# First memory piece split in the last layer's tail, next weights of block 2 shared out anew between engines; head and attention stages reordered

## What is computed

```python
for l in range(DEPTH):
    h = rms_norm(x, norm1_g[l]) * (1.0 + scale1) + shift1
    proj = h @ w_in[l]                    # latents c_q, c_kv, k_rope, and conv_u
    attn_out = mla_group(...)             # 4 heads, head norm, rope, softmax
    conv_out = conv_group(conv_u, ...)    # 31 taps by channel, layer norm, silu
    x = x + gate1 * (concat([attn_out, conv_out]) @ w_out[l])
    h2 = rms_norm(x, norm2_g[l]) * (1.0 + scale2) + shift2
    x = x + gate2 * expert_choice_ffn(h2, ...)   # 16 experts, 64 tokens each
```

## Time and profile before

| | us |
|---|---|
| median of 3 runs | 2667.12 |
| lowest and highest | 2662.14 and 2667.64 |
| the profiled execution | 2660.37 |
| its span | 2658.7 |

### The profile page before, as it was taken

The page is one execution under the profiler, slowest core; times in us unless marked ns, Lnnn a source line. Parts: engine busy times, 40 slices in busy tenths (PEclk is TensorE's granted clock), DMA queues, the critical chain, the costliest instruction groups (busy, mean ns, idle before and its releaser), DMA issues. The chain is left out here.

```text
span 2658.7 us, 31859 instructions
## 1 busy us (share of the span) xinstructions
PE 2481.6 (93%) x12913; PEld 1488.4 (56%) x12913; DVE 1124.8 (42%) x1732; ACT 851.1 (32%) x1161; POOL 298.8 (11%) x126
## 2 busy tenths in 40 slices
PE   6989799999997989799999998999999999989998
PEld 5734533333335735533333337887788777756665
DVE  4985312222223985312232225547521112356765
ACT  4245111111114245111111116556532234245553
POOL 0002000000000011000000005000244323300000
PEclk8999899999998989899999998999999999979999
DMA  9702579999999602499999995422223321149995
GB/s 339 273 1 83 203 303 409 410 409 410 409 408 329 225 1 95 191 353 409 410 410 410 410 402 148 149 89 80 80 74 97 131 80 48 48 176 371 358 353 207
DMA packets 276596, 650.48 MB, mean 245 GB/s; under 512 B 12144, under 2 KB 110718, under 8 KB 276222
## 3 DMA queue, kind: packets, MB, share of 16 engines
q1 hardware_dynamic: 273310, 638.87, 64.0%
q0 software_dynamic: 2592, 7.87, 0.8%
q10 hardware_dynamic: 576, 2.10, 0.2%
HBM read 641.99 MB, written 8.39 MB: 245 GB/s over the span
## 5 line engine op out<-in xcount | busy, mean ns | idle before, releaser
L790 PE MATMUL ps<-ring,scr 128*64 128x512 f32 x1952 | 426.9, 595 | 1.3 <-DMA ring<-in_w_up 1.3
L790 PEld LDWEIGHTS ps<-ring,scr 128*64 128x64 f32 x1952 | 138.9, 137 | 279.5 <-issue 274.6
L812 PE MATMUL ps<-ring,scr 128*64 128x512 f32 x1024 | 230.2, 603 | 1.4 <-ACT scr L1004 1.4
L1525 POOL TENSOR_TENSOR raw_r<-raw,w_high 128x2048 fp32r<-128x2048 f32 (+1 forms) x39 | 173.6, 4459 | 469.6 <-ACT w_high L1790 469.6
L1546 PE MATMUL ps<-x_high,w_high 128*128 128x512 f32 x464 | 187.5, 404 | 9.9 <-DVE y L2183 5.5
L1548 PE MATMUL ps<-x_high,raw_r 128*128 128x512 f32 x464 | 185.1, 399 | 0.0
L1547 PE MATMUL ps<-xT_r,w_high 128*128 128x512 f32 x464 | 184.5, 398 | 0.0
L1078 DVE SCALAR_TENSOR_TENSOR one_hot_T<-h_tok,convw,one_hot_T 128x512 f32<-128x512 f32 x240 | 170.5, 766 | 1.7
L490 POOL TENSOR_TENSOR one_hot_T_r<-hy,one_hot_T_r 128x1024 fp32r<-128x1024 f32 x16 | 38.5, 2404 | 1118.2 <-ACT one_hot_T_r L1016 1118.2
L1287 DVE TENSOR_TENSOR scr<-scr,ps 128x512 f32<-128x512 f32 x32 | 22.0, 688 | 314.6 <-PE ps L790 314.6
L2661 DVE TENSOR_TENSOR ring_r<-ring,ring_high 128x2048 fp32r<-128x2048 f32 x56 | 127.7, 2289 | 61.3 <-ACT ring_high L2539 61.2
(11 more groups left out here) (555 smaller groups left out, 4450.0 us busy)
## 6 DMA issues: line engine op xcount, KB each, us to landing
ring<-in_w_down SPq DMA_DIRECT2D x64, 2048.0 KB, 15.0
ring<-in_w_up SPq DMA_DIRECT2D x62, 2048.0 KB, 18.1
ring<-in_w_gate SPq DMA_DIRECT2D x60, 2048.0 KB, 14.7
ring<-in_w_up SPq DMA_DIRECT2D x56, 1024.0 KB, 7.7
ring<-in_w_ada SPq DMA_DIRECT2D x22, 2048.0 KB, 13.0
ring<-in_w_down SPq DMA_DIRECT2D x28, 1024.0 KB, 7.4
raw<-in_w_in SPq DMA_DIRECT2D x24, 1024.0 KB, 5.1
raw<-in_w_in SPq DMA_DIRECT2D x20, 512.0 KB, 4.7
```

Source lines behind the costliest of these rows:

```text
L790: mm = pe.matmul(ps[CAP * half:CAP * (half + 1), 1 + j // 2, :], x_e[:, at_x:at_x + CAP], weights[:, k, half * HALF:(half + 1) * HALF], st ...
L812: mm = pe.matmul(ps[CAP * half:CAP * (half + 1), 4, :], hidT[:, at_f:at_f + CAP], weights[:, k, half * HALF:(half + 1) * HALF], start=(j = ...
L1525: pool.tensor_tensor(dst, src, high.bitcast(F32), ALU.subtract).then_inc(w_ready, 1)
```

## The change

Seven things are done.

1. `TAPS_IN_TILE` has 1 and 5 taps where it had 4 and 2 (after input tiles 9 and 10). The 24 taps of the head stage become 16 before the ropes and 8 after them; `TAPS_IN_STEP` becomes 3, 3, 2, 4, 3, 4, 2.
2. Head stage on TensorE: the rotations move in between the last key tiles, into banks 4, 5, 0; the sums are taken in the order 0, 2, 3, 1, only the last waiting for all ten tiles; the value tiles are spread around the turning of the norms and the first key factor. ScalarE gets one dummy square root.
3. Attention: VectorE only inverts the row sum (new semaphore `inv_ready`); ScalarE scales the probabilities, after the exponential of the next step. The key factor and key norm come behind the inversion.
4. Nine matmuls of output tile 6 are done ahead, around the last transpose.
5. Tail of the last layer: the first four pieces are loaded in the order 0 to 3, ScalarE makes the high part of piece 0 there and GpSimd its low part, in place. VectorE no longer subtracts it in `second`.
6. Low parts in `second`: GpSimd 1 to 5, VectorE from 6 on. `w_ready` counts one less.
7. Piece 9's high part is made after the first of the four late key/value evictions instead of after all.

The core of the diff:

```diff
-TAPS_IN_TILE = (0, 5, 9, 9, 10, 10, 10, 10, 6, 4, 2, 4)
-TAPS_IN_HEADS = 24
-TAPS_IN_STEP = (4, 4, 4, 3, 3, 3)
+TAPS_IN_TILE = (0, 5, 9, 9, 10, 10, 10, 10, 6, 1, 5, 4)
+TAPS_IN_HEADS = (16, 8)
+TAPS_IN_STEP = (3, 3, 2, 4, 3, 4, 2)
+EARLY_OUT = 6
...
+def first_halves(M):
+    return M["ring2_r"][:, 3 * TT * D - 2 * SLOT:3 * TT * D - SLOT], M["h_tok_r"][:, 0:SLOT]
...
-    for i in (2, 3, 0, 1):
+    for i in range(SLOTS):
...
             with pool.If(l > DEPTH - 2):
+                pool.wait_ge(kv_split, 1)
+                pool.tensor_tensor(kv_low, h_tok[:, 0:SLOT], kv_high.bitcast(F32), ALU.subtract)
...
+                if i == 6:
+                    pe.wait_ge(qk_ev, 5)
+                    rotate(0, ROT_BANKS[0])
+                if i == 7:
+                    pe.wait_ge(qk_ev, 6)
+                    rotate(1, ROT_BANKS[1])
+            pe.wait_ge(qk_ev, 7)
+            rotate(2, ROT_BANKS[2])
...
-            for n in range(4):
+            for n in (0, 2, 3, 1):
+                if n == 1:
+                    pe.wait_ge(qk_ev, 10)
...
+            pe.wait_ge(roped, 3)
+            value_tile(0)
             pe.wait_ge(head_root, 1)
             for t in range(TT):
                 mm = pe.transpose(ps[:, 7, t * P:(t + 1) * P], head_rms[:, t * P:(t + 1) * P], ident)
             mm.then_inc(head_cols, 1)
+            value_tile(1)
+            value_tile(2)
...
             key_factor(0)
+            pe.wait_ge(qk_ev, 11)
+            value_tile(3)
...
                 j = i - 2
+                if j == 4 * HEADS - 1:
+                    early_output(0)
+                    early_output(1)
...
+                if j == 4 * HEADS - 1:
+                    early_output(2)
...
+                if 1 <= i <= 4 * HEADS:
+                    act.wait_ge(inv_ready, i)
+                    act.activation(prob[:, (i - 1) % 3, :], prob[:, (i - 1) % 3, :], ACT.Copy, scale=rrs[:, i - 1:i]).then_inc(prob_ready, 1)
...
             with act.If(l > DEPTH - 2):
+                act.wait_ge(ahead["slot_in"][0], 16)
+                act.activation(kv_high, h_tok[:, 0:SLOT], ACT.Copy).then_inc(kv_split, 1)
...
-                j = i - 1
-                if j >= 0:
-                    dve.wait_ge(exp_done, j + 1)
-                    step(dve.reciprocal(rrs[:, j:j + 1], rsum[:, j:j + 1]))
-                    step.settle()
-                    dve.tensor_scalar(prob[:, j % 3, :], prob[:, j % 3, :], rrs[:, j:j + 1], None, ALU.mult).then_inc(prob_ready, 1)
+                if i >= 1:
+                    dve.wait_ge(exp_done, i)
+                    dve.reciprocal(rrs[:, i - 1:i], rsum[:, i - 1:i]).then_inc(inv_ready, 1)
...
-            for i in range(1, KV_BEFORE + 1):
-                pool.wait_ge(w_ready, i)
+            for i in range(1, KV_BEFORE):
+                if i >= 2:
+                    pool.wait_ge(w_ready, i - 1)
...
-                    for i in range(2 * KV_BEFORE, 16):
+                    kv_kept(2 * KV_BEFORE)
+                    ahead(CH_H[1] - AHEAD)
+                    for i in range(2 * KV_BEFORE + 1, 16):
...
-            low_of(0)
...
-            next_low = [KV_BEFORE + 1]
+            next_low = [KV_BEFORE]
```

More of the change, by code:

```diff
@@ L632, in _ @@
                     elif n == 1:
-                        pe.matmul(out, key, sqs[:, 6 + h, :], start=False, stop=False)
+                        mm = pe.matmul(out, key, sqs[:, 6 + h, :], start=False, stop=True)
                     elif n == 2:
@@ L661, in _, with out_passes, early_output @@
             mm.then_inc(r_bias_mm, 1)
+            def out_passes(dt, n, kt, first, last):
+                tile = slice(dt * P, (dt + 1) * P)
+                pe.matmul(ps[:, dt, :], w_out_high[kt][:, tile], mix_high[:, kt, :], start=first, stop=False)
+                pe.matmul(ps[:, dt, :], w_out_high[kt][:, tile], mix_low[:, kt, :], start=False, stop=False)
+                return pe.matmul(ps[:, dt, :], w_out_low[:, kt, tile], mix_high[:, kt, :], start=False, stop=last)
+            def early_output(n):
+                kt = MIX_ORDER[n]
+                pe.wait_ge(w_out_ready, kt + 1)
+                pe.wait_ge(mix_ready, n + 1)
+                out_passes(EARLY_OUT, n, kt, n == 0, False)
             pe.wait_ge(qk_ev, 14)
-            pe.wait_ge(roped, 3)
             for i in range(4 * HEADS + 3):
@@ L707, in _ @@
             for dt in range(KT):
-                tile = slice(dt * P, (dt + 1) * P)
                 for n, kt in enumerate(MIX_ORDER):
+                    if dt == EARLY_OUT and n < 3:
+                        continue
                     if dt == 0:
@@ L1128, in _ @@
                     w_in_rest(9)
-            for _ in range(TAPS_IN_HEADS):
+            for _ in range(TAPS_IN_HEADS[0]):
                 next(conv)
@@ L1140, in _ @@
                 dve.wait_ge(roped, i + 1)
+            for _ in range(TAPS_IN_HEADS[1]):
+                next(conv)
             dve.wait_ge(head_cols, 1)
@@ L1782, in col @@
                 return vec[:, n:n + 1]
-            split = [0]
+            split = [1]
             def ahead(i):
@@ L1801, in kv_kept @@
                 act.activation(out, ps[:, bank, 0:2 * P], ACT.Copy).then_inc(kv_ready, 1)
-            for i in range(3):
+            for i in range(1, 3):
                 ahead(i - AHEAD)
```

72 lines of the change are left out of this document (40 added, 32 removed).

## The result

The changed kernel takes 2647.92 us (median of 6 runs, 2646.07 to 2650.9) against 2661.97 us before (6 runs, 2654.24 to 2667.64): a ratio of 0.9947, interval 0.9932 to 0.9961. It is faster by 0.5%, some 14 us. The forecast was 2650 and -17 us. The time was met, but the trace shows that one half of the gain, that of the head and attention stages, did not come about as described.

What follows compares the result with a forecast made beforehand. TensorE, busy 93% of the span, was taken to bound the kernel. Layers gain 4.5 us each, twice 9.0, block 2 8.0, together -17: 2667.1 becomes 2650 us, range 2640 to 2660.

Steps and rivals of the forecast that it cites:

- Part 1, taps: Before the latents' broadcast: moving three taps removes 2.0 of TensorE's 2.32 us wait; gain 2.0 us a layer.
- Part 2, head stage: Head stage: norms some 3 us sooner, but VectorE's same work only reordered; 0 us, ends -0.9 and +0.9.
- my walk: Stepping through attention's 19 rounds in both orders with traced durations; left idle times of 3.3 and 2.6 us, charged 1 us.
- Part 3, attention: Attention, scaling on ScalarE: 4.3 us sooner by step 7, 2.6 us wait at transpose 11; net -0.5 us a layer.
- Part 4, early matmuls: Around the last transpose: nine matmuls fill about 1.9 us idle and save 2.0 us a layer in the output projection.
- Part 5, tail: Tail of layer 1: added ScalarE and GpSimd work stays covered; cost 0, or 4.6 us if the cover were gone.
- Parts 6 and 7, block 2: Block 2: start gains 1.0 and 1.0 us, piece 9's earlier copy 6.0 after a new 1.2 us wait.
- "slower" one: Rival, chance 0.06: attention's score-to-transpose chain lowers TensorE's clock for good; decides from 8.5 us extra a layer, 2675 us.
- The first, fourth and fifth: Signs: latents' broadcast wait about 0.3 us; tail no longer; block 2 no head 1 wait over 1.5, new one about 1.
- The second: Sign: attention within 3.5 us of 81.5, ScalarE 10 us busier, VectorE 8 less, transpose 11 the longest wait, ended by ScalarE.
- The third: Sign: the output projection is 2 us shorter.
- signs of being wrong: ScalarE scalings over 0.8 us, attention's clock below 0.85, or GpSimd's new subtraction ending the tail.

Runs made afterwards that it cites:

- e12: Changed kernel with value tile 2 computed four times over, filling TensorE's wait ahead of the first key factor; 2637.85 us.
- e7: Kernel of e4 with the probabilities scaled on VectorE again; 2645.79 us.
- e4: Changed kernel with the head stage in the old order, all 24 taps ahead of the rotations; 2640.26 us.
- e10: Kernel of e5 without the nine early matmuls of the output projection; 2655.76 us.
- e9: Changed kernel with ScalarE's copy of piece 9 back behind the four memory value copies; 2656.29 us.
- e2: Kernel before with the taps, head stage, attention and early matmuls of the change, block 2 as before; 2658.09 us.
- e5: Changed kernel with 5 of the 8 late head-stage taps moved into the first seven attention steps; 2639.17 us.
- e11: Kernel of e5 with ScalarE's and VectorE's last attention round reordered: scaling 14 ahead of exponential 15, two output copies behind scaling 15; 2639.31 us.
- e3: Changed kernel with the probabilities scaled on VectorE as before; 2651.92 us.
- e1: Kernel before with the change's block 2 edits alone; 2652.66 us.
- e6: Kernel of e4 with the scaling of step 11 moved ahead of the root's table load on ScalarE; 2649.31 us.
- e8: Kernel before with only three taps moved from behind input tile 9 to behind input tile 10; 2659.05 us.

## Why the prediction held in its number and not in its sum

- **Part 1, taps: right.** Wait 2.32 to 0.33 us and 2.44 to 0.45; both 2.0.
- **Part 2, head stage: this is the step that failed.** "The same work in another order", with ends of -0.9 and +0.9, was worked out for VectorE, and for VectorE it holds: with the wait filled (e12) the first score starts 30.23 us after the head projections, as before (30.25). What was not asked is what TensorE does meanwhile. Its norms are ready 3 us sooner, so its small waits of 0.84 and 1.32 us become one of 2.48, and no term priced the clock behind it (0.50 for 17 us). It costs 2.4 us up to the first score and more behind it; e12 measures 7.5 and 6.8 us. I had charged the clock for the gaps that my walk found in attention, by the 3.07 us before 182.18, and not for the gap at a place I had called hidden.
- **Part 3, attention: mechanism right, net too good.** From the first score to the gathering the changed kernel is 4.1 us a layer longer. With the clock undisturbed (e12) that part is 0.9 and 0.3 us shorter, where -2.5 was forecast for parts 3 and 4 together. Against the kernel with VectorE's scaling (e7), 5.5 us were gained by transpose 7 and given back by the output projection. The price at step 11 was right (2.3 us for 2.6); the scaling took 0.71 us where 0.6 was taken; the last four steps, which were to keep 0.5 us of the gain, lose it: in e4 transposes 14 and 15 each come 0.93 us later than the spacing of before. The last value product does what was said, 3.70 instead of 5.40. (Of 4.3 us less 2.6 the prediction has 1.9 left; it is 1.7.)
- **Part 4, early matmuls: right** in size (1.4 and 3.0 us in e10, 2.0 forecast, with the clock of the last value product in it; the stretch from the output projection to the gathering is 1.5 us shorter).
- **Part 5, tail: right.** It is no longer (-0.7 us).
- **Parts 6 and 7, block 2: right, the first undersized.** Piece 9 gives 6.3 us for 6.0 and the new wait is 1.15 us for 1.2. The start gives 4.6 for 2.0 (e9 keeps the start alone): its two waits are 2.5, and the rest is that less of it runs at half clock.
- **The rivals.** The clock of the "slower" one (0.06), one that falls and stays down, is what happened, only behind the head stage instead of in attention's chain. By the traces the layers come out 9 us each worse than forecast (+6.6 and +6.5 for -2.5), which is past the 8.5 from which that rival decides; that the kernel is faster all the same is block 2 and what the sum below names. Its last figure is a slip: 2675 is 25 us more in all, not in each layer.
- **The signs.** The first, fourth and fifth came: waits of 0.33 and 0.45 us, a tail no longer, 1.15 us ahead of the third gating tile. The second did not: attention takes 87.2 us and not 81.5 within 3.5, and its longest wait is not that of transpose 11 (2.27 us) but one of 3.09 ahead of transpose 4, also ended by ScalarE. The third came at 1.5 us for 2. Of the signs of being wrong the clock is at its bound, 0.85.
- **The sum.** By its own parts, corrected for the traces, the changed kernel gains 11 us in block 2 and loses 9 in the layers. To come out at -14 it needs two things that no edit accounts for: the 7 us in places that nobody edited, and 4.6 us by which the two profiled executions differ less (9.5 us) than the medians (14.1). By the medians the head and attention part is worth -4.7 us (e2), half of the forecast's -9, and block 2 -10.1 (e1) for -8. And the kernel before was itself measured 5 us faster (2661.97) than the runs on which the forecast stood (2667.12), so that a gain 3 us too small gives a time 2 us under the 2650. Errors of opposite sign met: that the number was hit is luck.

The profile's rows allowed the missing step: a wait into which small ones merge is a wait to be priced for the clock, and the earlier trace rows had the price. The Trainium skill (TensorE: Matmul & The Clock Gate, What's actually happening) says that the slow clock is the default and that activity lifts it. By that I would have expected the level to rise soon once TensorE works without a pause, and would have charged the merged wait little; the trace has 16.00 us busy of 16 at 0.50, and the measurement decides.

e4, e5, e11 and e12 beat both kernels, at 2638 to 2640 us against 2648 and 2662. Of these e5 does no useless work and differs from the changed kernel in two lines of numbers.

## What to carry to other kernels

When a reordering lets TensorE arrive early at something that another engine delivers at the same time as before, count TensorE's waits after the change and not only the deliverer's time: several short waits that become one can put the clock at half, and that can cost a multiple of the wait (here 5 us in each layer by the medians, 7 by the traces, for 2.48). Before accepting such an order, look at the granted clock behind the merged wait; fill the wait or spread it if it is down. And where the gain of a part is a few us, measure the parts apart: here a sum of terms landed 2 us from the measured time with the head and attention stretch of each layer off by 9 us.

## What the runs showed of the hardware

- A wait of 2.48 us was followed by about 17 us at the lower level (1.2 GHz), in which TensorE was busy without a break (the changed kernel and e9 in both layers, e2 in layer 1). The same wait was followed by about 3 us of it in layer 0 of e2 and of e3, and by none in layer 1 of e3. A wait of 1.32 us had full clock behind it in both layers of before, e1, e4, e6 and e7 and in layer 1 of e8, and in layer 0 of e8 a mean of 0.57 over 16 us. The size of the wait alone doesn't say which, and nothing here settles what does. Without the wait (e12) the low level was absent behind the key factor in both layers.
- From the last scatter of layer 0 to the first matmul of layer 1 the traces of before and e10 take 19.9 and 20.4 us, all twelve others 16.1 to 17.2. The two have a second wait there, 3.71 and 4.02 us in the middle of the norm's sum, that the others lack; it is put down to issue, and its cause stays open. Its 3 to 4 us are as much as most edits here, and no edit was made there.
- Behind the gated stage of block 2, the stretch from TensorE's wait of 3.48 us (2236.50 in before) to its next long one, of 1.58 (2285.48), comes in two lengths: 48.8 to 49.0 us in before, e1, e2 and e7 to e11, 46.3 in the changed kernel, e3 to e6 and e12. In before the mean clock from 2235 to 2247 us is 0.72, in the changed kernel 1.00. With one trace of each kernel, an edit's effect of this size and the place where the clock happens to fall can't be told apart.
